# Reversed columns in the weight panels, and a moving operand read with step -1

## The chip, the cores and the metric

The kernel runs on one core of a Trainium2 chip. The metric is device time in microseconds (us) of one execution. Five engines share the core's on-chip memory: TensorE (PE, matmuls), VectorE (DVE), ScalarE (ACT), GpSimd (POOL) and SyncE (SP, which here issues DMA transfers). Each takes its instructions in order and waits for the others by semaphores. A matmul has a stationary operand, which is loaded into the array first (the trace shows that load as PEld), and a moving operand, whose columns stream through it; the results go to PSUM. In this kernel the weights of the network are the moving operand, 512 (or 256) columns at a time.

## The reference, cut to what matters

A decoder trunk of two layers over 256 tokens of width 1024, all in float32. Each layer has a feed-forward block, a mixing block (attention beside a convolution) and a second feed-forward block; every block is normalised and modulated by a conditioning vector.

```python
def swiglu(h, wg, wu, wd):
    return (jax.nn.silu(h @ wg) * (h @ wu)) @ wd
...
    for l in range(DEPTH):
...
        h = modulate(x, 0)
        x = x + 0.5 * gate(0) * swiglu(h, ffn_wg[l, 0], ffn_wu[l, 0], ffn_wd[l, 0])

        h = modulate(x, 1)
        z = h @ w_in[l]
        q, k, v, u, gates = jnp.split(z, SPLITS, axis=-1)
...
        y_conv = conv_module(u, conv_w[l], conv_b[l], conv_ln_g[l], conv_ln_b[l], conv_wo[l])
        g_attn, g_conv = jnp.split(gates, N_BRANCH, axis=-1)
        y = jax.nn.sigmoid(g_attn) * y_attn + jax.nn.sigmoid(g_conv) * y_conv
        x = x + gate(1) * (y @ w_out[l])

        h = modulate(x, 2)
        x = x + 0.5 * gate(2) * swiglu(h, ffn_wg[l, 1], ffn_wu[l, 1], ffn_wd[l, 1])
    return rms_norm(x, final_g)
```

## The kernel before

The host cuts all weight matrices into 200 panels, 100 for a layer (33 for each feed-forward block, 34 for the mixing block). A panel is 128 partitions by 2048 float32 columns: four chunks of 512 columns, each chunk holding 128 rows of the weight matrix (the input dimension on the partitions). The exception is the panel `M_V1` of each layer, which holds eight chunks of 256 columns.

SyncE loads the panels in order into `raw`, a ring of six (`load`, L279); the load of panel p waits until TensorE is done with panel p - 6 (`panel_done`).

There are two ways to use a panel:
- 176 panels are split. ScalarE writes the upper part of every number, rounded to fp32r (a float32 of which TensorE uses fewer bits, in a single pass), into `w_hi` (L708), and VectorE writes the rest into `w_lo` (L997), which lies over `raw`. TensorE then makes three fp32r matmuls for each product: upper by upper (L329), lower weight by upper activation (L330), upper weight by lower activation (L331). The helper is `three`.
- 24 panels stay whole (`is_whole`: the first four, and ten in each layer's mixing block). TensorE multiplies them as plain float32 out of `raw` (L348). The trace shows two records for each such matmul.

Three functions hand the columns of a panel to these matmuls: `k_half` (four chunks of 512, for the activations `hA`, `hB` or `hF`), `two_chunks` (down projections and the attention's output projection, with `mid`, `end` and `o` as the stationary operand), and `v1` (the panel `M_V1`, 256 columns at a time). In each, `c` is the slice of columns, and `t` the slice of tokens in the stationary operand. The other matmuls (transposes through `ident_sb`, attention scores L515 with their masks L506 to L509, probabilities by values L537) do not read panels.

The order of TensorE's work is written out by hand in `ffn` and `mix`, and the orders of ScalarE and VectorE follow the panels' order. Nothing in it depends on how a chunk's columns are laid out: `w_hi` and `w_lo` are made element by element, over all 2048 columns of a panel at once.

Of the kernel before, what the change touches and what calls it, by code (L numbers as in the profile page):

```python
# [13 lines left out]
P = 128  # L14
D = 1024
T = 256
DEPTH = 2
# [16 lines left out]
PW = 2048  # L34
FFN_PANELS = 3 * NJ
M_U, M_QK, M_V0, M_V1, M_G, M_AO, M_G3, M_CO, M_WO = 0, 8, 14, 16, 17, 23, 24, 26, 30
# [16 lines left out]
def is_whole(p):  # L53
    return p < FIRST_WHOLE or p % LAYER_PANELS - FFN_PANELS in WHOLE
# [5 lines left out]
def splits(p):  # L60

    return sum(q < p for q in SPLIT_PANELS)
# [6 lines left out]
def mix_base(l):  # L69
    return l * LAYER_PANELS + FFN_PANELS  # L70
# [41 lines left out]
def decoder_program(nc, x_in, c_row, g_row, params, rope, ident, mask, ada_w, weights, out):  # L112
    with ExitStack() as ctx:
# [152 lines left out]
        def acc(half, tt):  # L266
            return ps[:, 2 * half + tt, :]
# [57 lines left out]
        def _(pe):  # L325
# [7 lines left out]
            def parts(p):  # L333
                return w_hi[:, splits(p) % HI, :], w_lo[:, p % RAW, :]

            def ready(p):
                if is_whole(p):
                    pe.wait_ge(raw_in[p % RAW], 16 * (p // RAW + 1))
                else:
                    pe.wait_ge(lo_done, splits(p) + 1)  # L340

            def k_half(p, h, tt, b, out_ap, last=None):

                t = slice(tt * P, (tt + 1) * P)
                for i in range(4):
                    k, c = 4 * b + i, slice(512 * i, 512 * i + 512)
                    if is_whole(p):
                        mm = nc.tensor.matmul(out_ap, hF[:, k, t], raw[:, p % RAW, c], start=(k == 0), stop=(k == KC - 1))  # L348
                    else:
                        hi, lo = parts(p)  # L350
                        mm = three(out_ap, (h[0][:, k, t], h[1][:, k, t]), (hi[:, c], lo[:, c]), k == 0, k == KC - 1)
                if tt == 1:
                    mm.then_inc(panel_done, 1)
                elif last is not None:
                    mm.then_inc(last, 1)

            def both(p, h, b, banks):
                ready(p)
                for tt in range(TT):
                    k_half(p, h, tt, b, ps[:, banks + tt, :])  # L360

            def two_chunks(p, mids, tt, halves, start, stop, last=None):

                hi, lo = parts(p)
                for half in halves:
                    for kk in range(2):
                        c = slice(kk * D + half * 512, kk * D + half * 512 + 512)
                        mm = three(acc(half, tt), (mids[0][:, kk, :], mids[1][:, kk, :]), (hi[:, c], lo[:, c]),
                                   start and kk == 0, stop and kk == 1)
                if tt == 1 and 1 in halves:  # L370
                    mm.then_inc(panel_done, 1)
                elif last is not None and 1 in halves:
                    mm.then_inc(last, 1)
# [88 lines left out]
            def mix(l):  # L462
                base = mix_base(l)
                n = 3 * l + 1
# [24 lines left out]
                def v1(tt):  # L489
                    p = base + M_V1  # L490
                    hi, lo = parts(p)
                    t = slice(tt * P, (tt + 1) * P)
                    for k in range(KC):
                        c = slice(k * 256, k * 256 + 256)
                        mm = three(ps[:, 4 + tt, 0:256], (hA_hi[:, k, t], hA_lo[:, k, t]), (hi[:, c], lo[:, c]),
                                   k == 0, k == KC - 1)
                    if tt == 1:
                        mm.then_inc(panel_done, 1)
# [965 lines left out]
```

## Time and profile before

| | us |
|---|---|
| median of 3 runs | 1296.92 (1296.9 to 1297.17) |
| span of the profiled execution, first to last instruction | 1293.5 |
| TensorE busy in it | 1238.3 (96%) |
| VectorE busy | 965.1 (75%) |
| ScalarE busy | 547.3 (42%) |
| DMA, mean rate | 227 GB/s |

The profile is of one execution. Its span is 3.4 us under the median time; the difference lies ahead of the first and behind the last instruction. "Busy" counts the time covered by at least one record of an engine. Records of matmuls overlap, since the next one starts while the last one drains: the duration of a record is longer than its share of the engine's time, and the distance from one start to the next is what a matmul costs in a stream.

### The profile page before, as it was taken

The numbers are of one execution on the slowest core, as the hardware profiler recorded it, in microseconds if no ns is written. First come the engines' busy times: TensorE is split into PE (matmuls) and PEld (weight loads), VectorE is DVE, ScalarE is ACT, GpSimd is POOL, SyncE is SP. The second block draws the span as 40 slices with busy tenths as digits, with TensorE's granted clock in tenths as the row PEclk, the third lists the DMA queues.
The fourth block names the chain that finished last, engine by engine and source line by source line (L and its number), as shares of the span: only waits on it lengthen the run. The fifth ranks groups of instructions, "written<-read, shape, count | busy, mean of one in ns | idle before, by whom it ended". The sixth has DMA issues, their size and how long they took to land.

```text
span 1293.5 us, 13852 instructions
## 1 busy us (share of the span) xinstructions
PE 1238.3 (96%) x5448; PEld 957.3 (74%) x5448; DVE 965.1 (75%) x1341; ACT 547.3 (42%) x576; POOL 2.2 (0%) x5
## 2 busy tenths in 40 slices
PE   3999999999998999999999999999999899999997
PEld 2588887765765787888878888876676677888885
DVE  5698886699996576988668888669999856744443
ACT  3353344532345365344354443354233454644331
POOL 0000000000000000000000000000000000000000
PEclk9999999999999999999999999999999899999999
DMA  9989994454323339889747899454432334555540
GB/s 374 417 316 378 372 377 169 163 183 159 130 98 130 137 124 376 340 340 358 294 180 280 340 343 357 174 188 174 175 130 98 130 130 169 190 190 178 204 177 33
DMA packets 52913, 293.44 MB, mean 227 GB/s; under 512 B 6640, under 2 KB 6896, under 8 KB 27120
## 3 DMA queue, kind: packets, MB, share of 16 engines
q1 hardware_dynamic: 51120, 289.38, 60.0%
q10 hardware_dynamic: 1728, 3.17, 0.7%
q8 instruction: 43, 0.70, 0.2%
q14 instruction: 22, 0.18, 0.0%
HBM read 291.45 MB, written 1.07 MB: 226 GB/s over the span
## 4 chain that ended last, share of the span: by engine, by line
PE 89%; DVE 4%; DMA 3%; ACT 2%; issue 1%; SPq 0%; DVEq 0%
PE ps L329 23%; PE ps L331 23%; PE ps L330 23%; PE ps L348 13%; DMA raw<-in_weights 2%; PE ps L537 1%; PE ps L515 1%; PE ps L396 1%; DMA ada_raw<-in_ada_w 1%; DVE w_lo L997 1%; DVE hF L1084 1%; PE ps L526 0%; PE ps L485 0%; ACT L714 0%; DVE hA_lo L997 0%
## 5 line engine op out<-in xcount | busy, mean ns | idle before, releaser
L997 DVE TENSOR_TENSOR w_lo<-raw,w_hi 128x2048 fp32r<-128x2048 f32 x176 | 401.1, 2287 | 37.6 <-ACT w_hi L708 37.3
L708 ACT CAST w_hi<-raw 128x2048 fp32r<-128x2048 f32 x176 | 334.5, 1910 | 176.8 <-DMA raw<-in_weights 113.7
L329 PE MATMUL ps<-w_hi,hA_hi 128*128 128x512 f32 (+1 forms) x992 | 395.9, 399 | 5.8 <-DVE hA_lo L997 5.8
L331 PE MATMUL ps<-w_hi,hA_lo 128*128 128x512 f32 (+1 forms) x992 | 384.3, 387 | 0.0
L330 PE MATMUL ps<-w_lo,hA_hi 128*128 128x512 f32 (+1 forms) x992 | 383.6, 387 | 0.0
L329 PEld LDWEIGHTS ps<-w_hi,hA_hi 128*128 128x128 f32 x992 | 186.9, 188 | 49.8 <-issue 15.1
L331 PEld LDWEIGHTS ps<-w_hi,hA_lo 128*128 128x128 f32 x992 | 186.7, 188 | 39.0
L330 PEld LDWEIGHTS ps<-w_lo,hA_hi 128*128 128x128 f32 x992 | 187.0, 189 | 37.9 <-issue 2.9
L1186 DVE SCALAR_TENSOR_TENSOR work<-conv_in,par,work 128x256 f32<-128x256 f32 x480 | 193.9, 483 | 0.0
L1012 DVE SCALAR_TENSOR_TENSOR product<-ada_raw,c_bc 128x1024 f32<-128x1024 f32 x144 | 171.7, 1220 | 16.0 <-DMA ada_raw<-in_ada_w 15.6
L348 PE MATMUL ps<-raw,hF 128*128 128x512 f32 x384 | 172.0, 600 | 5.5 <-ACT hF L733 5.5
L348 PEld LDWEIGHTS ps<-raw,hF 128*128 128x128 f32 x384 | 72.1, 193 | 87.0 <-issue 86.8
L329 PE MATMUL ps<-w_hi,mid_hi 128*128 128x512 f32 x336 | 131.3, 391 | 2.3 <-DVE mid_lo L997 2.3
L330 PE MATMUL ps<-w_lo,mid_hi 128*128 128x512 f32 x336 | 130.8, 389 | 0.0
L331 PE MATMUL ps<-w_hi,mid_lo 128*128 128x512 f32 x336 | 130.8, 389 | 0.0
L997 DVE TENSOR_TENSOR mid_lo<-ps,mid_hi 128x512 fp32r<-128x512 f32 (+1 forms) x44 | 29.3, 667 | 106.7 <-ACT mid_hi L770 103.3
L763 ACT ACTIVATE act<-ps 128x512 f32<-128x512 f32 (+1 forms) x48 | 27.0, 563 | 136.6 <-PE ps L331 131.7
L329 PEld LDWEIGHTS ps<-w_hi,mid_hi 128*128 128x128 f32 x336 | 63.1, 188 | 15.9 <-DVE mid_lo L997 3.0
L770 ACT CAST mid_hi<-ps 128x512 fp32r<-128x512 f32 x40 | 23.4, 586 | 120.5 <-PE ps L396 120.5
L331 PEld LDWEIGHTS ps<-w_hi,mid_lo 128*128 128x128 f32 x336 | 63.1, 188 | 13.2
L330 PEld LDWEIGHTS ps<-w_lo,mid_hi 128*128 128x128 f32 x336 | 63.1, 188 | 12.9
L1100 DVE TENSOR_TENSOR mid<-act,ps 128x512 f32<-128x512 f32 (+1 forms) x48 | 30.9, 643 | 45.1 <-ACT act L763 45.1
(121 smaller groups left out, 749.7 us busy)
## 6 DMA issues: line engine op xcount, KB each, us to landing
raw<-in_weights SPq DMA_DIRECT2D x200, 1024.0 KB, 4.9
ada_raw<-in_ada_w SPq DMA_DIRECT2D x144, 512.0 KB, 7.5
gate_bc<-gate_scratch ACTq DMA_DIRECT2D x6, 512.0 KB, 6.4
x<-in_x_tok SPq DMA_DIRECT2D x1, 1024.0 KB, 7.6
out_tok<-xn_h SPq DMA_DIRECT2D x4, 256.0 KB, 2.2
c_bc<-in_c_row SPq DMA_DIRECT2D x1, 512.0 KB, 4.6
c_bc<-in_g_row SPq DMA_DIRECT2D x1, 512.0 KB, 5.6
mask_all<-in_mask SPq DMA_DIRECT2D x1, 416.0 KB, 16.6
```

Of the source, the lines that this page charges most:

```text
L329: nc.tensor.matmul(out_ap, stat[0], mov[0], start=start, stop=False)
L330: nc.tensor.matmul(out_ap, stat[0], mov[1], start=False, stop=False)
L331: return nc.tensor.matmul(out_ap, stat[1], mov[0], start=False, stop=stop)
L348: mm = nc.tensor.matmul(out_ap, hF[:, k, t], raw[:, p % RAW, c], start=(k == 0), stop=(k == KC - 1))
L396: mm = nc.tensor.transpose(ps[:, bank, c:c + P], mid[:, tt, kk * P:(kk + 1) * P], ident_sb[:])
L708: nc.scalar.copy(w_hi[:, s % HI, :], raw[:, p % RAW, :]).then_inc(hi_done, 1)
L763: nc.scalar.activation(act[:, tts[0]:tts[-1] + 1, :], ps[:, bank + tts[0]:bank + tts[-1] + 1, 0:256], ACT.Silu).then_inc(silu_done, 1)
L770: nc.scalar.copy(mid_hi[:], cols(bank)).then_inc(mid_hi_done, 1)
L997: return nc.vector.tensor_tensor(dst, whole, hi_part.bitcast(F32), ALU.subtract)
L1012: nc.vector.scalar_tensor_tensor(out=product[:, q % 2, :], in0=ada_raw[:, q % ADA_RING, :], scalar=1.0, in1=c_bc[:], op0=ALU.mult, op1=ALU ...
L1100: nc.vector.tensor_tensor(mid[:, c, :], act[:, c, :], ps[:, bank + tts[0]:bank + tts[-1] + 1, 256:512], ALU.mult).then_inc(mid_done, 1)
L1186: nc.vector.scalar_tensor_tensor(out=work[:, c, :], in0=conv_in[:, c, t:t + T], scalar=par[:, o:o + 1], in1=work[:, c, :], op0=ALU.mult, o ...
```

## The change

The host turns round the order of the columns inside each chunk: column 0 of a 512-wide chunk is stored last and column 511 first (the two panels `M_V1` are turned in chunks of 256). The kernel gives the matmuls the same chunk from its last column down to its first, with step -1, so each matmul streams the same numbers in the same order as before, and writes the same PSUM columns in the same order. `back` makes such a slice, and takes the place of the slices in `k_half`, `two_chunks` and `v1`. Every matmul on a panel is changed, and nothing else on the chip: the transfers, the splitting into `w_hi` and `w_lo`, the stationary operands, the outputs and all waits are as before.

```diff
@@ -333,6 +333,10 @@
             def parts(p):
                 return w_hi[:, splits(p) % HI, :], w_lo[:, p % RAW, :]
 
+            def back(first, n):
+
+                return slice(first + n - 1, first - 1 if first else None, -1)
+
             def ready(p):
                 if is_whole(p):
                     pe.wait_ge(raw_in[p % RAW], 16 * (p // RAW + 1))
@@ -343,7 +347,7 @@
 
                 t = slice(tt * P, (tt + 1) * P)
                 for i in range(4):
-                    k, c = 4 * b + i, slice(512 * i, 512 * i + 512)
+                    k, c = 4 * b + i, back(512 * i, 512)
                     if is_whole(p):
                         mm = nc.tensor.matmul(out_ap, hF[:, k, t], raw[:, p % RAW, c], start=(k == 0), stop=(k == KC - 1))
                     else:
@@ -364,7 +368,7 @@
                 hi, lo = parts(p)
                 for half in halves:
                     for kk in range(2):
-                        c = slice(kk * D + half * 512, kk * D + half * 512 + 512)
+                        c = back(kk * D + half * 512, 512)
                         mm = three(acc(half, tt), (mids[0][:, kk, :], mids[1][:, kk, :]), (hi[:, c], lo[:, c]),
                                    start and kk == 0, stop and kk == 1)
                 if tt == 1 and 1 in halves:
@@ -491,7 +495,7 @@
                     hi, lo = parts(p)
                     t = slice(tt * P, (tt + 1) * P)
                     for k in range(KC):
-                        c = slice(k * 256, k * 256 + 256)
+                        c = back(k * 256, 256)
                         mm = three(ps[:, 4 + tt, 0:256], (hA_hi[:, k, t], hA_lo[:, k, t]), (hi[:, c], lo[:, c]),
                                    k == 0, k == KC - 1)
                     if tt == 1:
@@ -1417,7 +1421,9 @@
             c = slice(512 * h, 512 * h + 512)
             panels[b + M_CO + 2 * h], panels[b + M_CO + 2 * h + 1] = k_halves(a["conv_wo"][l][:, c])
             panels[b + M_WO + h], panels[b + M_WO + 2 + h] = k_halves(a["w_out"][l][:, c])
-    weights = np.stack(panels)
+    narrow = [mix_base(l) + M_V1 for l in range(DEPTH)]
+    weights = np.stack([w.reshape(P, -1, 256 if p in narrow else 512)[:, :, ::-1].reshape(P, PW)
+                        for p, w in enumerate(panels)])
```

The program has the same instructions on each engine, in the same order and number (on TensorE each form of matmul stands as often as before), only the line numbers of what stands behind `back` are four higher.

## Rows read from the trace of the kernel before

**Rows 1.** The page's first part: busy time, share, instructions of each engine.
```profile
span 1293.5 us, 13852 instructions
PE 1238.3 (96%) x5448; PEld 957.3 (74%) x5448; DVE 965.1 (75%) x1341; ACT 547.3 (42%) x576; POOL 2.2 (0%) x5
```

**Rows 2.** The page's chain that ended last, by engine and by line.
```profile
PE 89%; DVE 4%; DMA 3%; ACT 2%; issue 1%; SPq 0%; DVEq 0%
PE ps L329 23%; PE ps L331 23%; PE ps L330 23%; PE ps L348 13%; DMA raw<-in_weights 2%; PE ps L537 1%; PE ps L515 1%; PE ps L396 1%; DMA ada_raw<-in_ada_w 1%; DVE w_lo L997 1%; DVE hF L1084 1%; PE ps L526 0%; PE ps L485 0%; ACT L714 0%; DVE hA_lo L997 0%
```

**Rows 3.** Groups of TensorE's matmuls, shapes apart: count, busy us, mean ns, idle.
```profile
L329 PE MATMUL ps<-w_hi,hA_hi 128*128 128x512 f32 x960 | 386.7, 403 | 5.8 <-DVE hA_lo L997 5.8
L348 PE MATMUL ps<-raw,hF 128*128 128x512 f32 x384 | 172.0, 600 | 5.5 <-ACT hF L733 5.5
L329 PE MATMUL ps<-w_hi,mid_hi 128*128 128x512 f32 x336 | 131.3, 391 | 2.3 <-DVE mid_lo L997 2.3
L329 PE MATMUL ps<-w_hi,hB_hi 128*128 128x512 f32 x64 | 26.0, 407 | 5.4 <-DVE hB_lo L997 5.4
L329 PE MATMUL ps<-w_hi,hA_hi 128*128 128x256 f32 x32 | 9.3, 290 | 0.0
L329 PE MATMUL ps<-w_hi,o_hi 128*128 128x512 f32 x16 | 7.1, 441 | 0.0
L329 PE MATMUL ps<-w_hi,end_hi 128*128 128x512 f32 x16 | 6.6, 414 | 0.8 <-DVE end_lo L997 0.8
```

**Rows 4.** Timeline of TensorE, 512 columns wide: start us, us, instruction (22 between).
```profile
61.22 0.39 PE L329 MATMUL ps<-w_hi,hA_hi 128*128 128x512 f32 x1
...
66.44 0.39 PE L331 MATMUL ps<-w_hi,hA_lo 128*128 128x512 f32 x1
```

**Rows 5.** Timeline of TensorE, 256 columns wide, first and last (35 between).
```profile
327.31 0.28 PE L331 MATMUL ps<-w_hi,hA_lo 128*128 128x256 f32 x1
...
331.63 0.28 PE L331 MATMUL ps<-w_hi,hA_lo 128*128 128x256 f32 x1
```

**Rows 6.** Timeline of TensorE, bf16 mask matmuls.
```profile
323.31 0.38 PE L507 MATMUL ps<-mask_all 128*128 128x512 bf16 x1
323.53 0.27 PE L509 MATMUL ps<-mask_all 128*128 128x256 bf16 x1
```

**Rows 7.** Stretches: span, busy us (x) by engine, granted clock, DMA share, GB/s.
```profile
core 0: us, PE busy (x) PEld busy (x) DVE busy (x) ACT busy (x) POOL busy (x), PEclk, DMA share, GB/s
60.00:67.00 7.00, 7.00 (x35) 5.78 (x34) 4.83 (x6) 4.68 (x3) 0.00 (x0) 1.00 0.88 364
444.00:447.40 3.40, 3.40 (x10) 2.63 (x9) 1.38 (x1) 0.00 (x0) 0.00 (x0) 0.54 0.20 84
```

**Rows 8.** The chain in order of time, 444.4 to 448: start us, us, what.
```profile
444.45 0.43 PE ps L330
...
447.01 0.43 PE ps L330
```

**Rows 9.** The chain in order of time, whole panels and longest transfers.
```profile
251.26 6.87 PE ps L348 x16
...
374.29 4.85 DMA raw<-in_weights
...
493.57 13.56 DMA raw<-in_weights
...
1001.63 4.89 DMA raw<-in_weights
```

**Rows 10.** Waits of SyncE's queue: us in total, times, longest us.
```profile
SPq L279 <- PE ps L331: 901.8, 169, 15.4
SPq L279 <- PE ps L348: 178.0, 23, 13.2
```

**Rows 11.** Weight loads of the stationary operand, L331: count, duration min/median/max in ns.
```profile
L331 PEld LDWEIGHTS ps<-w_hi,hA_lo x992: 187/188/334, 61.5 to 1277.8; 128*128 128x128 f32 x199
```

## The prediction, made before the changed kernel ran

> **What bounds the kernel now.** I read the page's first part to find the busiest engine: TensorE is busy for 1238.3 of 1293.5 us, the next one, VectorE, for 965.1 [rows 1]. A high share alone doesn't make an engine the bound, so I read the chain of work that ended last: TensorE holds 89% of it, and 82% of the whole span is four lines, L329 to L331 (the fp32r matmuls on split panels) and L348 (the float32 matmuls on whole panels) [rows 2]. These four lines are the ones that the change rewrites. The kernel waits for TensorE nearly everywhere, so whatever a panel matmul gains or loses is gained or lost by the end of the run, thousands of times over.
>
> How many there are: the groups of L329 with 512 columns have 960, 336, 64, 16 and 16 instructions, 1392 in all [rows 3]; L330 and L331 have as many, which makes 4176 (174 split panels by 4 chunks by 2 token tiles by 3 gives the same). With 256 columns it is 3 x 32 = 96. L348 has 384 records, two for each of 192 float32 matmuls [rows 3].
>
> What one costs is the distance between starts, not the length of its record. In a stream of 512-wide fp32r matmuls the first starts at 61.22 us and the 24th at 66.44 us [rows 4]: 5.22 / 23 = 0.227 us. With 256 columns it is (331.63 - 327.31) / 36 = 0.120 us [rows 5]. The difference, 0.107 us for 256 columns, is 2.4 columns per ns: at the full clock (granted 1.00, the 2.4 GHz level [rows 7]) one column enters per cycle, and some 0.227 - 0.213 = 0.013 us is fixed per matmul. A float32 record takes 6.87 / 16 = 0.429 us [rows 9]. So the panel matmuls hold 4176 x 0.227 + 96 x 0.120 + 384 x 0.429 = 948 + 12 + 165 = 1125 us of the 1293.5; the rest is other matmuls and about 55 us in which TensorE had nothing to do (1293.5 - 1238.3).
>
> **The change, part by part.** The median run, 1296.92 us, is 3.4 us over the profiled span, and the change touches nothing outside it, so I add differences to the median.
>
> The host's reversal happens before the launch and costs the device nothing. The transfers move the same 1024 KB panels in the same pattern. ScalarE's and VectorE's splitting goes over the whole panel element by element, with step +1 as before: zero. The products, the order in which they enter the array, and the order in which PSUM is written are the same numbers in the same order, so nothing that depends on data or on the output side changes. No wait is added, removed or moved, and every engine has the same instructions in the same order. These have one answer, zero, and none needs cover from other work.
>
> What is left is one unknown: the rate at which TensorE's reading side delivers a chunk from its last column down. No instruction in the trace reads a moving operand with a negative step, nor with any innermost step other than 1, so I bound it. At the low end the descending read keeps one column per cycle: 0.227 us, difference 0. At the high end it delivers one float32 in two cycles, which would look like the stretch in which the clock was granted at half, 0.54 over the window with its edges [rows 7]: there the starts are (447.01 - 444.45) / 6 = 0.427 us apart [rows 8], so +0.200 us for 512 columns. Below zero: the bf16 mask matmul of 512 columns has its successor 0.22 us behind it [rows 6], against 0.227 for fp32r; if turning round the read took away that difference, it would be 0.007 us x 4272 = 30 us at most, with no reason for it.
>
> I take 0. Rows 6 and rows 4 speak for it: with 2 bytes for each column and with 4 bytes for each column the matmuls come 0.22 and 0.227 us apart. A doubled amount of data costs next to nothing, and when the array's clock halves the distance becomes twice 0.213 [rows 8]. So the array's clock sets the pace, and the reading side keeps up with four-byte elements. A descending read touches exactly the same bytes, four neighbours at a time, only from the other side. That doesn't exclude a read path that handles only ascending neighbours together, which is why the high end stays.
>
> The stationary load is untouched and lies behind the stream: 188 ns for a load against 227 ns from start to start [rows 11, 4], so its cover stays as it is.
>
> Two places of the Trainium skill bear on this. "Advanced Engine Details and Errata", section "SBUF Cachelines", says that SBUF has 16-byte lines and that a reader keeps full speed as long as it hits a line at least twice before leaving it. Descending float32 columns hit each line four times, as ascending ones do, so by that rule the sum is +0; a rule that penalised each access would fit none of rows 4 and 5. The same page's "2x-1p Requirements" counts a step of -1 as a unit step for VectorE's paired mode. No run here shows either for TensorE; if the opposite held (a descending read taken one element at a time) the sum would be the high end above.
>
> **The rivals.**
>
> *Same (forecast).* Reading direction is free: 1296.9 + 0 = 1296.9 us. One limit of it: 0.2% is 2.6 us, which over 4272 fp32r matmuls is 0.0006 us each. A difference of one nanosecond in each matmul would already be 4 us. That is what I grant as uncertainty above, and half of it below.
>
> *Half rate (slower).* The reading side fetches neighbours together only when the address rises, and a descending chunk comes at one element per two cycles. Place: every panel matmul. Price: 4176 x 0.200 = 835 us, plus 96 x 0.107 = 10 us for the narrow ones. Back from it: the transfers that the chain waits for, 4.85 + 13.56 + 4.89 = 23 us [rows 9], since SyncE's loads wait for TensorE's releases (901.8 + 178.0 us of waiting, 192 times) [rows 10] and would have more time to land. That gives 1297 + 845 - 23 = 2119 us. If a float32 record, which now takes 0.429 us, doubles too, it is 384 x 0.43 = 165 us more, 2284 without and 2307 with none of the 23 us given back. I would name 2140 us, as I think a float32 record, already at two cycles a column, is less likely to suffer. It decides from any extra of 0.0006 us per matmul upward, since nothing hides TensorE. For it: four-byte elements at one per cycle are the most demanding stream here. Against it: the argument of the rows above.
>
> *A fixed cost (slower, small).* The read of a descending chunk starts with a different address, and setting it up or crossing from one chunk to the next costs as much again as the 0.013 us that now stands fixed at each matmul: 4272 x 0.013 = 57 us, 1354 us. Between 0 and this lies every small price per instruction. Nothing in the trace asks for it.
>
> *Not what it says.* The compiler might turn the negative step into something else, such as an ascending read with reversed output, or chunks cut into pieces. The first would not change the read at all and gives 1297 us; the second would show as more matmuls, and the changed program has exactly as many. I count it within the forecast.
>
> *Faster.* The 0.007 us above, 1267 us, or a smaller part of it. Only for completeness.
>
> **How the numbers follow.** Same: 0.80. Half rate: 0.13, since the only argument against it is by analogy from ascending reads, and a whole class of hardware takes shortcuts for rising addresses. A fixed or small price: 0.05. Faster: 0.02. The predicted time is that of the likeliest, 1296.9 us. The range has to leave out no more than 0.2: the same case alone holds 0.80, so it runs from 1296.9 - 2.6 = 1294.3, rounded to 1294, up to 1296.9 + 4272 x 0.001 + rounding = 1302, which takes in the lowest part of the small prices. The half rate, far off at 2119 to 2307, is left out whole. A measurement of this kernel can tell about 0.2% from no change. Slower by more than that: 0.13 + 0.05 = 0.18; within it 0.80; faster 0.02.
>
> **What would show it.** If I am right, the starts of 512-wide fp32r matmuls stay 0.227 us apart and those of 256 wide ones 0.120, 16 records of L348 still take 6.87 us, TensorE's busy time stays within 2 us of 1238, and the chain has the same shares. If half rate is right, the same distances are 0.427 and 0.227 us with the granted clock still at 1.00, TensorE nears 98% of a span above 2100 us, and the waits of ScalarE and VectorE for TensorE grow by hundreds of us. If there is a fixed price, the 512-wide and the 256-wide distances grow by the same amount, while a price per column grows them two to one. What would make me wrong without any of this is a clock that is granted lower for longer stretches, in which the distances at full clock would be unchanged and the granted clock in the stretches would tell.

## The result and the profile after

The changed kernel takes 1320.9 us (median; 1316.54 to 1321.85) against 1296.91 us before: a ratio of 1.0184, 95% interval 1.0165 to 1.0203. The forecast was 1296.9 us with a range up to 1302. It was wrong: the kernel became 24 us, 1.8%, slower.

The first part of the page of the changed kernel, which answers to [rows 1]:

```profile
span 1320.0 us, 13852 instructions
PE 1266.0 (96%) x5448; PEld 960.4 (73%) x5448; DVE 965.6 (73%) x1341; ACT 545.7 (41%) x576; POOL 2.2 (0%) x5
```

The span grew by 26.5 us and TensorE's busy time by 27.7; the other engines did the same work in the same time. TensorE's idle time went from 55.2 to 54.0 us. So all of it is in TensorE's own instructions, and next to nothing was given back in waits. The chain of work has the shares of [rows 2], but for "issue" with 2% instead of 1%:

```profile
PE 89%; DVE 4%; DMA 3%; ACT 2%; issue 2%; SPq 0%; DVEq 0%
```

Now the distances between starts, which the prediction had asked to look at. The timeline of TensorE in the changed kernel, the same 24 matmuls of 512 fp32r columns as in [rows 4] (22 rows left out):

```profile
62.37 0.40 PE L329 MATMUL ps<-w_hi,hA_hi 128*128 128x512 f32 x1
...
67.74 0.40 PE L331 MATMUL ps<-w_hi,hA_lo 128*128 128x512 f32 x1
```

5.37 / 23 = 0.2335 us, where it was 0.227. The groups by form say the same for all such matmuls, and say which kinds are not touched (count, busy us, mean ns, idle):

```profile
L330 PE MATMUL ps<-w_lo,mid_hi 128*128 128x512 f32 x336 | 133.5, 397 | 0.0
L352 PE MATMUL ps<-raw,hF 128*128 128x512 f32 x384 | 174.2, 606 | 5.5 <-ACT hF L737 5.5
L329 PE MATMUL ps<-w_hi,hA_hi 128*128 128x256 f32 x32 | 9.2, 288 | 0.0
```

The record of this group of fp32r matmuls of 512 columns has grown by 8 ns on average (389 before, 397 now). The one of 256 columns has not grown (290 before, 288 now). L352, the float32 matmul, reads 606 against 600, but in the chain 16 records of it still take 6.87 us, as in [rows 9]:

```profile
257.01 6.87 PE ps L352 x16
```

The group's mean varies between kernels of either direction (`layout_only`, which reads ascending, has 604; `whole_narrow`, whose float32 matmuls descend, has 600; both are described below). In the chain the first 64 of these records take 30.34 us, and 29.61 before. That 0.7 us is the clock: each kernel begins this stretch at the half level (the changed one has a granted clock of 0.50 from 24 to 29.6 us), where the starts are 853 ns or more apart instead of 429: four such distances before and six after. The first records, merged by the timeline, before and after:

```profile
24.04 8.13 PE L348 MATMUL ps<-raw,hF 128*128 128x512 f32 x14 [5.47 <-ACT hF L733]
...
24.34 8.01 PE L352 MATMUL ps<-raw,hF 128*128 128x512 f32 x12 [5.46 <-ACT hF L737]
```

The granted clock is given as 0.91 from 24 to 55 us in the changed kernel. For the kernel before it is given as 1.00 there, which the distances contradict: the clock records of that run begin at 27.9 us only. The stretches of the changed kernel (length, then busy us (x) of PE, PEld, DVE, ACT, POOL, then granted clock, DMA share, GB/s):

```profile
24.00:55.00 31.00, 30.66 (x68) 13.54 (x68) 20.44 (x33) 9.74 (x15) 0.00 (x0) 0.91 1.02 413
60.00:67.00 7.00, 7.00 (x31) 5.64 (x30) 4.95 (x6) 4.78 (x3) 0.00 (x0) 1.00 0.92 356
```

At the full clock the steady fp32r distance is 16 cycles longer: 226.7 ns are 544 cycles of 2.4 GHz, 233.3 ns are 560. Where the clock is granted at half, the changed kernel shows the 0.427 us of [rows 8] again, with nothing added. A stretch of it (as above), and two matmuls inside with four between them, 2.13 / 5 = 0.426 us:

```profile
453.00:456.20 3.20, 3.20 (x9) 2.44 (x8) 0.85 (x1) 0.00 (x0) 0.00 (x0) 0.50 0.07 28
453.51 0.63 PE L329 MATMUL ps<-w_hi,hB_hi 128*128 128x512 f32 x1
...
455.64 0.63 PE L331 MATMUL ps<-w_hi,hB_lo 128*128 128x512 f32 x1
```

Taking all distances behind fp32r matmuls of 512 columns that lie between 215 and 250 ns: 4030 of them before, mean 227.5 ns, and 4020 after, mean 233.4 ns. 5.85 ns x 4030 = 23.6 us is nearly the 24.0 us between the medians. The sum of all 4175 distances behind such matmuls, at either clock, grew from 990.2 to 1013.8 us.

### The profile page after: what moved, and what is told of

Its sections match the earlier page's. It is cut to its first block, busy times and chain, and to the rows that moved or that the text cites. A ratio compares the mean times of both kernels' runs of the same rounds, so it can differ in the third digit from the quotient of the medians.

```text
span 1320.0 us, 13852 instructions
## 1 busy us (share of the span) xinstructions
PE 1266.0 (96%) x5448; PEld 960.4 (73%) x5448; DVE 965.6 (73%) x1341; ACT 545.7 (41%) x576; POOL 2.2 (0%) x5
## 4 chain that ended last, share of the span: by engine, by line
PE 89%; DVE 4%; DMA 3%; ACT 2%; issue 2%; SPq 0%; DVEq 0%
PE ps L329 24%; PE ps L331 23%; PE ps L330 23%; PE ps L352 12%; DMA raw<-in_weights 2%; PE ps L541 1%; PE ps L519 1%; PE ps L400 1%; DMA ada_raw<-in_ada_w 1%; DVE hF L1088 1%; PE ps L489 0%; ACT L718 0%; DVE w_lo L1001 0%; PE ps L530 0%; DVE hA_lo L1001 0%
## 5 line engine op out<-in xcount | busy, mean ns | idle before, releaser
L329 PE MATMUL ps<-w_hi,hA_hi 128*128 128x512 f32 (+1 forms) x992 | 402.3, 406 | 5.1 <-DVE hA_lo L1001 5.1
L331 PE MATMUL ps<-w_hi,hA_lo 128*128 128x512 f32 (+1 forms) x992 | 391.3, 394 | 0.0
L330 PE MATMUL ps<-w_lo,hA_hi 128*128 128x512 f32 (+1 forms) x992 | 391.1, 394 | 0.0
L331 PEld LDWEIGHTS ps<-w_hi,hA_lo 128*128 128x128 f32 x992 | 186.8, 188 | 43.8
L352 PE MATMUL ps<-raw,hF 128*128 128x512 f32 x384 | 174.2, 606 | 5.5 <-ACT hF L737 5.5
L352 PEld LDWEIGHTS ps<-raw,hF 128*128 128x128 f32 x384 | 72.8, 195 | 88.5 <-issue 88.4
L329 PE MATMUL ps<-w_hi,mid_hi 128*128 128x512 f32 x336 | 134.1, 399 | 2.0 <-DVE mid_lo L1001 2.0
L330 PE MATMUL ps<-w_lo,mid_hi 128*128 128x512 f32 x336 | 133.5, 397 | 0.0
L331 PE MATMUL ps<-w_hi,mid_lo 128*128 128x512 f32 x336 | 133.5, 397 | 0.0
L331 PEld LDWEIGHTS ps<-w_hi,mid_lo 128*128 128x128 f32 x336 | 63.2, 188 | 15.2
```

What stands on the lines that cost most here:

```text
L329: nc.tensor.matmul(out_ap, stat[0], mov[0], start=start, stop=False)
L330: nc.tensor.matmul(out_ap, stat[0], mov[1], start=False, stop=False)
L331: return nc.tensor.matmul(out_ap, stat[1], mov[0], start=False, stop=stop)
```

## The experiments

The question at the start was where the price sits: in the fp32r matmuls of 512 columns alone, or in all. The theories on its cause were the reads of the next stationary operand (theory 1), a price for each column (2), and the place of the first column in its line (3). The first four runs bear on these.

### Only one kind of matmul descends

`whole_narrow` turns round only the chunks of the float32 and of the 256-wide matmuls, `wide_only` only those of the fp32r matmuls of 512 columns.

```diff
@@ whole_narrow, against the changed kernel @@
-                    k, c = 4 * b + i, back(512 * i, 512)
+                    k, c = 4 * b + i, back(512 * i, 512) if is_whole(p) else slice(512 * i, 512 * i + 512)
...
-                        c = back(kk * D + half * 512, 512)
+                        c = slice(kk * D + half * 512, kk * D + half * 512 + 512)
...
-                        for p, w in enumerate(panels)])
+                        if is_whole(p) or p in narrow else w for p, w in enumerate(panels)])
```

> Only the 192 float32 matmuls (384 records, 512 columns) and the 96 fp32r matmuls of 256 columns read descending; the 4176 fp32r matmuls of 512 columns ascend, on panels that the host leaves as they were. Theory that the fp32r matmuls of 512 columns carry the loss: 1297 us (0 from the float32 ones, 0.1 to 0.3 us gained by the narrow ones). Theory that every descending matmul costs: 384 x 6.7 ns = 2.6 us more, 1299.5 us or above.

> Only the 4176 fp32r matmuls of 512 columns read descending. They are 6.67 ns further apart in the trace of the changed kernel, which is 27.8 us; of this some is given back in waits. Theory that they carry the loss: 1297 + 24 to 28 = 1321 to 1325 us, the same as the changed kernel. A rival, that the float32 and narrow matmuls or the clock share the loss, expects 1315 us or less.

`whole_narrow`: 1296.08 us, ratio 1.0004 (0.9993 to 1.0016), no change. The mean of its descending float32 records is the 600 ns of before:

```profile
L352 PE MATMUL ps<-raw,hF 128*128 128x512 f32 x384 | 172.1, 600 | 5.7 <-ACT hF L737 5.7
```

`wide_only`: 1318.62 us, ratio 1.0171 (1.0152 to 1.0189). That is under the 1321 to 1325 expected and above the rival's 1315; within the intervals of the two ratios it is the whole loss. It sits in the 4176 fp32r matmuls of 512 columns, whose distances have the mean of the changed kernel, 233.4 ns.

### The layout without the step

`layout_only` keeps the host's reversed chunks and reads them ascending (the edit against the changed kernel).

```diff
-                    k, c = 4 * b + i, back(512 * i, 512)
+                    k, c = 4 * b + i, slice(512 * i, 512 * i + 512)
...
-                        c = back(kk * D + half * 512, 512)
+                        c = slice(kk * D + half * 512, kk * D + half * 512 + 512)
...
-                        c = back(k * 256, 256)
+                        c = slice(k * 256, k * 256 + 256)
```

> The host reverses the chunks as in the changed kernel, but the matmuls read them ascending, so the columns of every product come out reversed within a chunk and what is computed is not the reference. All theories on the reading side expect the time before, 1297 us, and 226.7 ns between 512-wide matmuls. If the time were 1310 to 1322 us, the order of the numbers in memory would be the cause and not the step.

1296.31 us, ratio 0.9999 (0.9989 to 1.0008). The order of the numbers in memory costs nothing; the order in which TensorE reads them does.

### The matmuls by themselves

`micro1` is a small program (like the four that follow it, it ran once): blocks of 24 back-to-back matmuls, made with the same two `w` tiles and `h` tiles in the same hi, lo, hi pattern. `mv(i, n, step, off)` gives n columns with that step, shifted by `off` columns. Lines such as these:

```python
            for i in range(24): MM(ps[:, 1, :], st(i), mv(i, 512, 1), **kw(i))
            for i in range(24): MM(ps[:, 2, :], st(i), mv(i, 512, -1), **kw(i))
...
            for i in range(24): MM(ps[:, 3, :], st(i), mv(i, 512, 2), **kw(i))
```

> This kernel leaves the whole decoder out: it loads two weight panels, makes fp32r, bf16 and float32 copies, and runs blocks of 24 matmuls (12 in float32), one form of operand in each block, each block on a line of its own; its output is zeros. What counts is the distance between starts at the full clock. Known from the two traces: 512 fp32r columns, 226.7 ns ascending and 233.3 ns descending. Theory 1 (stationary load): the stream loses cycles while the next stationary operand is read from the same memory, 13.3 ns (32 cycles of 2.4 GHz) ascending and 20 ns (48) descending. Then a stationary operand of 64 or of 32 columns lowers both (ascending to some 220 and 217 ns, descending to some 223 and 218 ns) and the difference of 6.7 ns shrinks in step; bf16, with half the bytes to load, shows at most half of it. Theory 2 (price per column): the descending read costs 0.013 ns more for each column, whatever the stationary operand: 512 to 448 to 384 to 320 to 256 columns differ by 6.7, 5.8, 5.0, 4.2, 3.3 ns, and a stationary operand of 32 columns still shows 6.7 ns. Theory 3 (alignment of the first column): the extra comes from where the first read falls in its line; a chunk shifted by 1 or 2 columns changes the descending distance by several ns. If neighbours are fetched together only in rising order, step +2 would cost as much as or more than step -1; if the direction alone counts, step +2 stays at 226.7 and step -2 is at 233.3.

Timeline of TensorE in it, the first and the last of 24 for 512 columns ascending (L85), descending (L86), and with step 2 (L95):

```profile
30.12 0.39 PE L85 MATMUL ps<-w_hi,h_hi 128*128 128x512 f32 x1
...
35.34 0.39 PE L85 MATMUL ps<-w_hi,h_lo 128*128 128x512 f32 x1
35.56 0.40 PE L86 MATMUL ps<-w_hi,h_hi 128*128 128x512 f32 x1
...
40.94 0.40 PE L86 MATMUL ps<-w_hi,h_lo 128*128 128x512 f32 x1
...
72.22 0.63 PE L95 MATMUL ps<-w_hi,h_hi 128*128 128x512 f32 x1
...
82.66 0.63 PE L95 MATMUL ps<-w_hi,h_lo 128*128 128x512 f32 x1
```

5.22 / 23 = 0.227, 5.38 / 23 = 0.234 and 10.44 / 23 = 0.454 us: the kernel's numbers come back with nothing else running. The mean distances in ns of the blocks, without the first three and the last of each:

| fp32r columns | ascending | descending |
|---|---|---|
| 512 | 226.7 | 233.4 |
| 448 | 202.9 | 206.4 |
| 384 | 174.5 | 177.7 |
| 320 | 146.7 | 146.7 |
| 256 | 119.6 | 118.4 |
| 512, step 2 and -2 | 453.1 | 466.6 |
| 512 and 1 column late | 238.2 | 235.6 |
| 512 and 2 columns late | 233.3 | 235.6 |
| 512 and 64 columns late | 226.7 | 233.4 |
| 512, stationary operand of 64 columns | 230.3 | 233.3 |
| 512, stationary operand of 32 columns | 231.5 | 233.3 |
| 512 in bf16 | 215.8 | 215.8 |
| 512 in float32, per record | 429.2 | 429.2 |

A price for each column (theory 2) falls: it expected 4.2 ns at 320 columns and 3.3 at 256, and there is none. Theory 1 in its simple form falls too: loading fewer stationary columns does not take the price away, it raises the ascending distance. Theory 3 expected several ns on the descending side from a shift by 1 or 2 columns; it is 2.2 there, and 6.6 to 11.5 on the ascending side. Nor is it the alternation of tiles: the same stationary columns each time give 226.7 and 233.3 ns, and `w_hi` alone as the stream (in `micro2`) 226.6 and 233.3. What stays is that ascending reads are not one thing: shifted by two columns, an ascending read costs as much as a descending one. The half rate of the prediction exists, but at step 2. The price of the step does not grow steadily with the width: `micro2` has 3.5 ns at 480 columns, 3.1 at 496, 1.6 at 504 and 3.5 at 508.

Two more blocks read the chunk in groups of four columns (16 bytes). With rising groups and falling columns inside them (innermost step -1) the distance is 226.7 ns (L116 below); with falling groups and rising columns inside them it is 233.3 (L117):

```profile
209.00 0.40 PE L116 MATMUL ps<-w_hi,h_hi 128*128 128x512 f32 x1
...
214.22 0.39 PE L116 MATMUL ps<-w_hi,h_lo 128*128 128x512 f32 x1
214.45 0.40 PE L117 MATMUL ps<-w_hi,h_hi 128*128 128x512 f32 x1
...
219.82 0.40 PE L117 MATMUL ps<-w_hi,h_lo 128*128 128x512 f32 x1
```

### Which part of the reversal costs, in the whole kernel

`inner4` reverses the columns inside each group of four and leaves the groups in rising order; `outer4` reverses the order of the groups and leaves the columns in each rising. Both compute what the kernel before computes. The expectations name two theories that the next section tests further: by A the place of the stream's first column counts, by B the order in which the groups of 16 bytes ("lines") are visited.

```diff
@@ inner4, against the kernel before @@
+            def fours(ap):
+                return ap.rearrange("p (c n) -> p c n", n=4)
+
+            def back(ap):
+                return fours(ap)[:, :, ::-1]
...
-                        mm = three(out_ap, (h[0][:, k, t], h[1][:, k, t]), (hi[:, c], lo[:, c]), k == 0, k == KC - 1)
+                        mm = three(fours(out_ap), (h[0][:, k, t], h[1][:, k, t]), (back(hi[:, c]), back(lo[:, c])), k == 0, k == KC - 1)
...
@@ outer4, against inner4 @@
-                return fours(ap)[:, :, ::-1]
+                return fours(ap)[:, ::-1, :]
```

> All panel matmuls read with an innermost step of -1, but in groups of four columns (16 bytes): the host reverses the columns within each group of four, and the matmul takes the groups in rising order and the four columns of each falling. Micro1 had 226.7 ns for this form. Theories A and B: 1297 us, within 0.2% of before. A theory by which the step of -1 itself costs (any change of the innermost direction) expects 1320 us.

> The other half: the host reverses the order of the groups of four columns in a chunk, and the matmul takes the groups from the last to the first and the four columns of each rising, so no innermost step is negative. Micro1 had 233.3 ns for this form. Theories A and B: 1319 to 1322 us, the loss of the changed kernel. A theory by which the negative innermost step costs expects 1297 us.

`inner4`: 1296.46 us, ratio 1.0001 (0.9989 to 1.0013). `outer4`: 1319.86 us, ratio 1.0193 (1.0176 to 1.021). Page of `outer4`, first part:

```profile
PE 1262.0 (96%) x5448; PEld 958.1 (73%) x5448; DVE 965.7 (73%) x1341; ACT 545.5 (41%) x576; POOL 2.2 (0%) x5
```

The distances say the same: 227.5 ns in `inner4`, as before, and 233.4 in `outer4`, as in the changed kernel. The negative step as such is free; the whole loss comes from visiting the groups of 16 bytes from high to low.

### Place, order, or the stationary operand

> No decoder, blocks of 24 fp32r matmuls of one form each, output zeros, as in micro1. There the step of -1 cost 6.7 ns at 512 columns, nothing at 320, nothing in bf16 or float32, and groups of four columns cost 226.7 ns when the groups rise and the columns in them fall, 233.3 ns the other way round. Theory A (place of the first column): what counts is how far the first column lies from the start of some block of memory. Then ascending chunks that start 4, 8 or 16 columns late cost 233 ns until the shift is a whole block (64 cost 226.7), falling groups of 16 or 64 with rising columns cost 226.7, and a shift by 4 to 32 changes a descending chunk. Theory B (order of lines): what counts is whether the 16-byte lines are visited upward or downward. Then an ascending chunk costs 226.7 at every shift by a multiple of 4, a descending one 233.3, and falling groups of 16 and 64 with rising columns lie between 226.7 (128 and more) and 233.3 (4). Theory C (stationary load): what counts is how the reads of the next stationary operand meet those of the stream, since a narrower one changed the ascending distance in micro1 (230 and 232 ns). Then a shift of the stationary operand by 4 to 64 columns moves the distances by several ns, and some shift could bring the ascending one under 226.7. Matmuls that alternate in direction: A and B expect 226.7 and 233.3 in turn, mean 230; a cost at the turn from chunk to chunk expects another number.

`micro2` gave no theory its full due. (Theory C: what counts is how the reads of the next stationary operand meet those of the stream.) Ascending chunks that start 4, 8, 16 or 32 columns late: 231.9, 233.4, 228.7 and 232.6 ns, where theory B wanted 226.7. Descending ones at 4, 8 and 16: 233.3; at 32, 236.8, and at 3, no multiple of four, 240.2. Groups of 16 that fall with rising columns: 233.3, against theory A's 226.7; of 64 and 128 columns: 227.7 and 226.6. Shifting only the stationary operand by 4 or 16 columns: 233.3 and 233.4 ascending, 233.4 and 233.3 descending. That is what theory C expects; a shift by 64 columns gives 227.8 and 233.3. Alternating directions: 230.4, the mean, though the distances do not alternate between 227 and 233 as expected but between 228 and 232. And one order was far worse than a plain reversal, falling columns in groups of 16 that rise (L101):

```profile
91.53 0.43 PE L101 MATMUL ps<-w_hi,h_hi 128*128 128x512 f32 x1
...
97.66 0.43 PE L101 MATMUL ps<-w_hi,h_lo 128*128 128x512 f32 x1
```

6.13 / 23 = 0.267 us.

> No decoder, blocks of 24 fp32r matmuls with 512 columns, output zeros, as in micro1 and micro2. Ascending and descending blocks, with the moving operand shifted by 0 to 60 columns in steps of 4 (stationary in place), then the stationary operand shifted likewise (moving in place), then both by the same amount; last, stationary operands of 1, 8 and 16 columns. Theory C, in the form that micro2 suggests (the reads of the stream and of the next stationary operand meet in one memory, and what counts is how far apart the two addresses are, modulo 64 columns or 256 bytes): both shifted by the same amount keeps 226.7 ns ascending and 233.3 descending at every shift, while shifting one alone moves the ascending distance within 226 to 236 ns. Theory A (place of the first column of the stream alone): shifting both costs as much as shifting the moving operand alone (228 to 234 ns ascending), and shifting the stationary one alone is free, which micro2 speaks against. A stationary operand of one column leaves next to nothing to meet: theory C expects under 226 ns, near the 215.8 ns of bf16, in both directions, if the amount that is loaded counts; a fixed price per matmul expects 227 to 233 ns still.

`micro3` scans the shifts. The forms that `micro2` had too come back within 0.7 ns. Ascending, with both operands shifted by the same amount, the distance is 227.8 ns at 8, 16, 24 and so on up to 56 columns, and 229.9 ns at 4, 12, 20 and so on up to 60: it depends hardly at all on where the two lie together. With one of them shifted alone it is 229 to 235 ns at 28 of the 30 shifts, and 226.7 at the other two, 60 columns, either way. Descending, 40 of the 45 shifted blocks lie between 233.2 and 233.5 ns, and the other five at 236.7 or 236.8. Timeline, ascending and in place (L90), ascending with the stationary operand 16 columns late (L109), ascending with both 16 columns late (L124):

```profile
30.24 0.39 PE L90 MATMUL ps<-w_hi,h_hi 128*128 128x512 f32 x1
...
35.45 0.39 PE L90 MATMUL ps<-w_hi,h_lo 128*128 128x512 f32 x1
...
136.07 0.39 PE L109 MATMUL ps<-w_hi,h_hi 128*128 128x512 f32 x1
...
141.44 0.39 PE L109 MATMUL ps<-w_hi,h_lo 128*128 128x512 f32 x1
...
219.43 0.39 PE L124 MATMUL ps<-w_hi,h_hi 128*128 128x512 f32 x1
...
224.69 0.39 PE L124 MATMUL ps<-w_hi,h_lo 128*128 128x512 f32 x1
```

5.21, 5.37 and 5.26 us for 23 distances. A stationary operand of a single column gives 231.7 ns ascending and 233.3 descending, so the number of columns loaded is not what counts: that part of theory C falls.

### The same loss without any descending read

`before_phase64` is the kernel before, with the tiles that hold the stationary operands 64 bytes later against the panels. With the first edit everything that lies behind `hA` moves by the same 64 bytes, other engines' tiles too; the panels, `w_hi`, `w_lo`, `x` and `hF` stay.

```diff
-        hA_at = room(2 * KC * T * 4, 0)
+        hA_at = room(2 * KC * T * 4, 64)
...
-        att_at = room(16896, 0)
+        att_at = room(16896, 64)
...
-        gates_at = room(16384, 0)
+        gates_at = room(16384, 64)
```

> The kernel before, ascending reads and unchanged panels; only the three places in memory that hold the stationary operands of the panel matmuls (and what shares them) start 64 bytes, 16 columns, later against the panels, modulo 512 bytes. Theory C: micro2 had 233.4 ns for an ascending stream with its stationary operand 16 columns late, so 4176 x 6.7 ns = 28 us more, of which the changed kernel showed 24 to 26 in the end: 1319 to 1322 us, with no descending read anywhere. A theory by which the direction or the place of the stream alone counts expects 1297 us.

1316.59 us, ratio 1.0155 (1.0133 to 1.0177). Its 24 matmuls of the stretch shown above (timeline):

```profile
61.27 0.40 PE L329 MATMUL ps<-w_hi,hA_hi 128*128 128x512 f32 x1
...
66.64 0.39 PE L331 MATMUL ps<-w_hi,hA_lo 128*128 128x512 f32 x1
```

5.37 us again, as in the changed kernel. Over the whole trace the mean is 233.3 ns, as there, and the sum of the distances 22.2 us above that of the kernel before, of a span that is 22.0 us longer; VectorE and ScalarE are as busy as before (965.1 and 546.0 us). So the distances account for the whole loss, none is left for the other tiles that moved, and the 64 bytes lengthen the distances as much as the descending read does. The time lies a little under the 1319 to 1322 us expected.

The narrow matmuls go the other way. In the kernel before, 36 distances behind matmuls of 256 columns took 4.32 us, 0.120 each [rows 5]. Here 36 of them (35 rows left out) take 4.08 us, 0.113 each:

```profile
332.17 0.28 PE L331 MATMUL ps<-w_hi,hA_lo 128*128 128x256 f32 x1
...
336.25 0.28 PE L331 MATMUL ps<-w_hi,hA_lo 128*128 128x256 f32 x1
```

The same shift that costs 6 ns at 512 columns saves 6 ns at 256. This kernel has only 96 such matmuls.

`after_phase64` makes the same edit in the changed kernel.

> The changed kernel, descending reads, and also the stationary operands 64 bytes later against the panels, as in the run that did this to the kernel before. Theory C, with the distances of micro3: descending with the stationary operand 16 columns late is 233.4 ns, as without the shift (233.3), so the shift adds nothing: 1318 to 1322 us. Were the two prices independent, they would add: 1297 + 24 + 20 = 1341 us.

1317.35 us, ratio 1.0173 (1.0154 to 1.0192), with a mean distance of 233.3 ns. The two prices do not add. For 512 columns the distance before was the good case of one alignment and one order, and losing either loses it; once it is lost, the other makes no difference.

### Other orders, other types, and what the stream meets

> No decoder, blocks of 24 matmuls (12 in float32), output zeros, as before. First bf16 ascending and descending with the stationary operand shifted by 0, 8, 16, 32 and 64 columns, then float32 with it shifted by 16. If the price comes from two 4-byte reads meeting at one column per cycle, bf16 (half the bytes) stays at 215.8 ns and float32 (two cycles a column) at 429.2 at every shift and in both directions; if shifts alone disturb a stream, they move too. Then fp32r: a stationary operand that takes every second column, expected like a shifted one, 227 to 234 ascending and 233 descending if the order of lines matters. Last, the lines of a chunk in other orders that a host could lay out: woven from 2, 4, 8, 32 strands of 4 columns or 2 and 8 of 8 columns, and neighbouring lines swapped in twos, fours and eights. Theory C (the two reads meet in the same parts of memory) says that an order that goes back to the same 256-byte phase again and again (strands 64 or more columns apart) costs far more than 233 ns, as groups of 16 falling columns did with 266.6. If any order gives less than 226.6 ns, it would be a kernel faster than the one before; I expect none.

In `micro4` bf16 stays at 215.8 ns in both directions and at all shifts of the stationary operand, and float32 at 429.2 in both directions at the one shift tried, 16 columns. A stationary operand with step 2 costs 233.3 ns ascending and 233.4 descending. Chunks woven from 2, 4 and 8 strands of four columns cost 249.7, 268.2 and 276.2 ns, from 32 strands 227.5; from 2 and 8 strands of eight columns 243.2 and 259.8. Lines of four columns swapped in twos, fours and eights cost 233.2, 266.6 and 240.0. Neighbouring groups of 16 columns swapped in twos and fours cost 236.8 and 233.4. The four ascending control blocks gave 226.6, 227.7, 227.8 and 226.7. No order came under 226.6 ns, so none of those tried would make a kernel faster than the one before. The woven form with 8 strands:

```profile
137.93 0.45 PE L130 MATMUL ps<-w_hi,h_hi 128*128 128x512 f32 x1
...
144.28 0.45 PE L130 MATMUL ps<-w_hi,h_lo 128*128 128x512 f32 x1
```

> No decoder, output zeros. In each block an fp32r matmul and a bf16 matmul, both with 512 columns and the bf16 one ascending, follow each other 24 times. During an fp32r stream only a bf16 stationary operand is then loaded, and during a bf16 stream an fp32r one; the last two blocks load a bf16 operand of one column. Forms of the fp32r stream: ascending, descending, ascending with its stationary operand 16 columns late, ascending and itself 16 columns late, falling in groups of 16 that rise (266.6 ns in micro2), woven from 8 and from 2 strands of 4 columns (276 and 250 ns in micro4). If the meeting of two fp32r reads makes the price, the distance behind an fp32r matmul is near 216 to 220 ns in all forms, and all differences go. If the order of the lines in the stream alone makes it, the distances behind the fp32r matmuls repeat those of the pure blocks, 227, 233, 233, 229, 267, 276 and 250 ns, though the shift of the stationary operand can then do nothing. Something between, order dependent but smaller, would say that any load can meet the stream and that an fp32r load meets it more.

In `micro5` the start of a bf16 matmul is recorded 40 ns ahead of the fp32r one behind it, so only a pair can be read, from one fp32r start to the next. Pure blocks would give 226.7 + 215.8 = 442.5 ns; the ascending pair takes 460.0. The other forms, against that pair: descending +4.5 ns (464.5), stationary operand 16 columns late 0.0, the stream itself 16 columns late +6.7, groups of 16 falling columns +33.4, woven from 8 strands +46.7, from 2 strands +13.3. In pure blocks these were +6.7, +6.7, +2.1, +40, +50 and +23. The last two blocks, with a bf16 stationary operand of one column, take 740 and 738 ns for a pair, where something else sets the time.

Ten pairs each, ascending (L112) and with the stationary operand 16 columns late (L114), 4.60 us both times:

```profile
35.33 0.58 PE L112 MATMUL ps<-w_hi,h_hi 128*128 128x512 f32 x1
...
39.93 0.58 PE L112 MATMUL ps<-w_lo,h_hi 128*128 128x512 f32 x1
...
54.76 0.58 PE L114 MATMUL ps<-w_hi,h_hi 128*128 128x512 f32 x1
...
59.36 0.58 PE L114 MATMUL ps<-w_lo,h_hi 128*128 128x512 f32 x1
```

So most of the price of an order stays when a bf16 operand is loaded beside the fp32r stream. The place of the fp32r stationary operand no longer matters when it is loaded beside a bf16 stream. The place of the stream itself matters more here than in the pure block (6.7 ns against 2.1), so these pairs do not clear the load of the bf16 operand. The outcome is nearest to the third of the expectation.

## Why the prediction was wrong

**Which engine, which instructions, how many: right.** TensorE bounds the kernel, the panel matmuls are on its path, and a nanosecond in each is 4 us. The prediction's own threshold, 0.6 ns in each fp32r matmul, was passed ten times over by an effect too small to see in a record of 0.39 us.

**The parts at zero: right.** The host's order, the transfers, and the splitting cost nothing (`layout_only`, 0.9999). The float32 matmuls cost nothing, whether they descend or not, and the narrow ones gave 1.5 ns each (119.9 before, 118.4 after), 0.1 us in all.

**The step that failed** is "I take 0" for the descending read. It stood on the bf16 and the fp32r distances, 0.22 and 0.227 us [rows 4, 6]: the data doubles and the distance hardly moves, hence the reading side keeps up with spare room. The 0.013 us between 0.227 and 512 columns at 2.4 per ns had been worked out and was called a fixed cost of a matmul. It was not fixed. bf16 has 215.8 - 213.3 = 2.5 ns of it and fp32r 13.3, and it goes to 20 ns when the groups of 16 bytes fall, and to 63 ns in the worst order tried (276.2). Those 13.3 ns were a sign that the fp32r stream has no spare room. Rows 8 held another. At the half clock the distance is 0.427 us, the bare 512 columns at 1.2 per ns. A cost that every matmul pays would have stayed there, at 13 ns or more; it was gone, and in the changed kernel the other 6.7 ns are gone there too. The prediction read these rows as proof that the reading side keeps up. They show it for the half clock only. A row with 0.22 in it has too few digits to show it, and the difference of 0.007 us stood in the text as a possible gain, never as a sign of a possible loss.

**The argument "the same bytes, four neighbours at a time, only from the other side"** was right inside a group of four (`inner4`, 1.0001) and wrong for the order of the groups (`outer4`, 1.0193). The rule of the Trainium skill that stood beside it ("Advanced Engine Details and Errata", "SBUF Cachelines": 16-byte lines, full speed from two hits a line) agrees with `inner4`, where each line is hit four times and the distance is unchanged; it is silent on the order in which lines are visited. Taken as a forecast of +0 it was wrong, since the descending chunk hits each line four times and still costs 6.7 ns. At step 2 fp32r hits each line twice, which by that rule is full speed, and took 453 ns instead of 227: there the measurement contradicts the page.

**The rivals.** The nearest was the fixed cost, named at 13 ns for each matmul, 1354 us at most, and given 0.05. Its sign and size came nearest: a small price per instruction. Its mechanism, another first address, was not it: `inner4`, too, starts a chunk at another address (its fourth column) and costs nothing. Its test in the prediction, that 512 and 256 columns grow by the same amount, came out as neither of the two alternatives there, 6.7 ns and -1.2 ns (`micro1`). The half rate was wrong for step -1; step 2 shows it (453.1 ns). Its 2140 us followed from no sum (the sums give 2119, 2284 and 2307), which changed nothing. The range was cut at 1 ns per matmul, with no row that made 1 ns the limit; the row distance of 13 ns was there and should have been its upper end.

**The sum.** With the measured term it closes: 5.85 ns x 4030 = 23.6 us from the distances, 24.0 between the medians. The profiled run shows 26.5: 23.7 in the sum of these distances, of which some 1.4 is the clock (21 distances of 426 or 427 ns at the half level against 14 before), 0.7 in the first stretch, also the clock, and 2.1 that was not taken apart.

**What stays open.** Why rising groups from an aligned start are the good case is not settled. Shown is that the distance depends on the order of the 16-byte groups and, ascending, on the place of the stationary operand relative to the stream; that neither a step of -1 nor the shifts tried act in bf16 or float32; and that moving the fp32r stationary operand does nothing when it is loaded beside a bf16 stream. Whether a load has to be under way for the order to cost is open: no block runs an fp32r stream without one. Parts of the memory that two readers, or two reads in close succession, can't use together would explain this, but no run here identifies them. The Trainium skill's page "TensorE: Matmul & The Clock Gate" (Part 2, "Step-by-step: what each phase is for") says that the stationary load has a read port of its own and takes nothing from the running matmul. In bf16 and float32 the runs agree (215.8 ns at every shift of the stationary operand, 429.2 at the one shift tried); in fp32r they don't (226.7 to 233.4 ns by a shift of the stationary operand alone, 16 columns).

## What to carry to other kernels

Between "the same speed" and "half the speed" there are prices of a few nanoseconds per instruction, and in a kernel that repeats one instruction 4000 times these are the result. Before calling a path free, compute the distance between starts to 0.1 ns from a long row of them and compare it with columns divided by clock: a remainder that differs between types (2.5 ns for bf16, 13.3 for fp32r here) is a sign that the stream already pays for its reads, and that changing their order or place can cost more. A remainder that vanishes at the half clock is another. With fp32r operands and 512 columns, read the moving operand upward in memory and start stationary and moving tiles at the same place modulo 256 bytes. That period rests on one shift of each operand (64 columns: 226.7 ns for the stream, 227.8 for the stationary operand); a shift of 60 columns was free too, and the other shifts of one operand cost 2 to 8 ns. Both shifted together cost 1 to 3 ns. At 256 columns measure first, since there a shift of 64 bytes gained 6 ns.

## What the hardware showed that was not expected

- An fp32r stream of 512 columns costs 226.7 ns ascending and aligned, 233.3 descending, and up to 276.2 in an order of 16-byte groups that looks harmless. In bf16 (215.8) and float32 (429.2 per record) the step of -1 changes nothing.
- Step -1 inside groups of four columns is free. Step 2 doubles the time, 453.1 ns.
- Moving the stationary tiles, and all that lies behind them, by 64 bytes made the kernel 1.55% slower. The matmuls of 512 columns went from 227.5 to 233.3 ns and those of 256 from 119.9 to 113.7.
- At the half clock the fp32r distance is 0.427 us ascending and descending; both the 13.3 ns and the 6.7 ns show at the full clock only.
- The steady distances are 544 and 560 cycles of 2.4 GHz; less regular forms settle into repeating patterns (for instance 245 and 255 ns in turn), and the same ascending block can settle at 226.6 or 227.7 ns depending on what ran ahead of it.
